# Extra products of two constants on TensorE in a fused transformer and expert kernel, and both heads' value products in one PSUM bank

## What is computed

```python
def first_block(x, c, ...):                        # in the kernel: ffn1 ... ffn2
    h = rms_norm(x, g_pre_ffn1) * (1 + sc1) + sh1
    x = x + 0.5 * gt1 * rms_norm(swiglu(h, ...), g_post_ffn1)
    u = rms_norm(x, g_pre_mix) * (1 + sc2) + sh2
    y = hybrid_mixer(u, ...)                       # index scores, dil and dsa attention, gates, w_o
    x = x + gt2 * rms_norm(y, g_post_mix)
    h = rms_norm(x, g_pre_ffn2) * (1 + sc3) + sh3
    return x + 0.5 * gt3 * rms_norm(swiglu(h, ...), g_post_ffn2)

# the index scores of a block of 128 queries, 8 heads of 32 features
logits = jnp.einsum('bqhe,bse->bqhs', qi, k_idx) * idx_scale
iscore = jnp.einsum('bqh,bqhs->bqs', wi, jax.nn.relu(logits))
_, sel = lax.top_k(where(causal, iscore, -inf), 128)       # the keys that dsa attends to

# each attention (dil, dsa, mla), per head and block of queries
p = softmax(where(mask, q @ k.T * scale, -inf)); o = p @ v

def second_block(x, c, ...):                       # in the kernel: in2 ... peer
    h = rms_norm_2(x, g_norm1) * (1.0 + sc1) + sh1
    mixed = concat(mla_group(h @ w_in ...), retention_group(...)) @ w_out
    x = x + gt1 * mixed
    h2 = rms_norm_2(x, g_norm2) * (1.0 + sc2) + sh2
    x = x + gt2 * peer(h2, w_query, sub_keys, expert_u, expert_v)
    return rms_norm_2(x, g_final)
```

## Time and profile before

| | us |
|---|---|
| median of three runs | 2976.38 |
| lowest and highest run | 2975.09, 2978.75 |
| span of the profiled execution, first to last instruction | 2975.7 |

### The profile page before, as it was taken

One profiled execution on the slowest core, in us unless ns is written; L12 is line 12 of the kernel. 1 busy time (PEld: TensorE's weight loads), 2 busy tenths in 40 slices (PEclk: granted clock), 3 DMA queues, 4 the chain that ended last, 5 costly groups with the idle time before them and its releaser, 6 DMA issues. The chain is left out here.

```text
span 2975.7 us, 37340 instructions
## 1 busy us (share of the span) xinstructions
PE 2827.2 (95%) x14083; PEld 2381.1 (80%) x14083; DVE 2012.1 (68%) x3510; ACT 1071.7 (36%) x1578; POOL 908.6 (31%) x603
## 2 busy tenths in 40 slices
PE   7999989888899999998989899999999999999998
PEld 6787878855687778887756789998899999898776
DVE  7754356376633783336445399899589888998887
ACT  3222232253523321223234335555433333333333
POOL 0000000040310000000014236676777777775230
PEclk9999999977999999999989999999999999999999
DMA  8963312101132873532111135665989898988994
GB/s 282 286 225 106 114 55 94 59 1 38 52 97 72 265 258 113 84 115 80 45 33 47 70 107 180 191 198 187 344 312 336 314 332 310 344 313 316 347 354 187
DMA packets 305769, 540.11 MB, mean 182 GB/s; under 512 B 19032, under 2 KB 199612, under 8 KB 287932
## 3 DMA queue, kind: packets, MB, share of 16 engines
q1 hardware_dynamic: 211936, 375.09, 37.5%
q0 software_dynamic: 36864, 134.23, 12.4%
q10 hardware_dynamic: 56796, 28.45, 3.5%
HBM read 498.90 MB, written 38.82 MB: 181 GB/s over the span
## 5 line engine op out<-in xcount | busy, mean ns | idle before, releaser
L183 PE MATMUL ps<-query_h_hi,expert_u_hi 128*128 128x384 f32 (+1 forms) x1152 | 399.5, 347 | 2.4 <-DVE query_h_lo L843 2.1
L183 PE MATMUL ps<-query_h_lo,expert_u_hi 128*128 128x384 f32 (+1 forms) x1152 | 395.5, 343 | 0.0
L2408 POOL TENSOR_TENSOR expert_u_lo<-feat,expert_u_hi 128x1024 fp32r<-128x1024 f32 x142 | 350.0, 2466 | 114.3 <-ACT expert_u_hi L2670 112.9
L183 PE MATMUL ps<-expert_v_hi,expert_w_hi 128*128 128x512 f32 x768 | 303.1, 395 | 8.3 <-DVE expert_w_lo L2576 5.8
L183 PE MATMUL ps<-expert_v_hi,expert_w_lo 128*128 128x512 f32 x768 | 301.2, 392 | 0.0
L183 PE MATMUL ps<-expert_v_lo,expert_w_hi 128*128 128x512 f32 x768 | 300.7, 392 | 0.0
L2581 DVE TENSOR_TENSOR expert_v_lo<-peer_s,expert_v_hi 128x1024 fp32r<-128x1024 f32 x128 | 204.5, 1598 | 121.3 <-ACT expert_v_hi L2678 120.5
L183 PE MATMUL ps<-ffn_h_hi,ffn_w_hi 128*128 128x512 f32 x704 | 279.2, 397 | 4.3 <-DVE ffn_h_lo L523 2.0
L183 PE MATMUL ps<-ffn_h_hi,ffn_w_lo 128*128 128x512 f32 x704 | 275.4, 391 | 0.0
L183 PE MATMUL ps<-ffn_h_lo,ffn_w_hi 128*128 128x512 f32 x704 | 275.3, 391 | 0.0
L246 DVE TENSOR_TENSOR ffn_w_lo<-ffn_w_raw,ffn_w_hi 128x2048 fp32r<-128x2048 f32 x64 | 146.6, 2290 | 158.4 <-ACT ffn_w_hi L230 158.4
(11 more groups left out here) (501 smaller groups left out, 6401.3 us busy)
## 6 DMA issues: line engine op xcount, KB each, us to landing
feat<-in_expert_u_blocks SPq DMA_DIRECT2D x64, 1024.0 KB
peer_s<-in_expert_v_blocks SPq DMA_DIRECT2D x64, 1024.0 KB
gate_rows<-expert_gates SPq DMA_DIRECT2D x31, 768.0 KB
ffn_w_raw<-in_w_down SPq DMA_DIRECT2D x22, 1024.0 KB, 5.0
ffn_w_raw<-in_w_gate SPq DMA_DIRECT2D x43, 512.0 KB, 7.5
ffn_w_raw<-in_w_up SPq DMA_DIRECT2D x43, 512.0 KB, 8.7
gate_rows<-in_w_mod SPq DMA_DIRECT2D x21, 1024.0 KB, 7.3
gate_rows<-in_w_ada SPq DMA_DIRECT2D x18, 1024.0 KB, 6.3
```

The source lines that it names most:

```text
L183: return nc.tensor.matmul(out, lhsT, rhs, start=start, stop=stop, skip_group_check=True)
L2408: nc.gpsimd.tensor_tensor(u_lo[:, n % 2, :, :], u_raw[:, n // 2 % 2, n % 2, :, :], u_hi[:, n % 2, :, :], ALU.subtract).then_inc(u_lo_done, 1)
```

## The change

`warm_up` becomes `keep_clock`, which issues n f32 products of the constants, 128 columns wide unless said otherwise, into a PSUM region that nobody reads at that time. It is called

- in `stage_norm_close` (three times in the program): 8 products ahead of the transposes of tile 2, 5 ahead of those of tile 3;
- in `stage_norm_queries`: 6 ahead of the transposes of tile 3 and 8 at the end;
- at the end of `stage_swiglu` (ffn1, ffn2) and of `stage_project_split` where the next stage is loaded early (o1, o2): 12, behind a wait for the PSUM bank to have been read;
- in the attention pairs (three times): after the scores of each of the first four pairs 4, 4, 1, 1 products of 256 columns in dil, one each in dsa and mla; and 6 of 256 columns at the end of TensorE's program;
- in the index scores: one after each of the 24 products, and 6 at the end.

Bank 7 becomes free for that in the attention by putting the values of both heads of a pair into bank 6.

```diff
-def warm_up(nc, b, n):
+def keep_clock(nc, b, n, bank, at=0, width=P):
...
     for _ in range(n):
-        mm(nc, b.ps[:, 7, :], b.const("identity"), b.const("decay_mask"), True, True)
+        mm(nc, b.ps[:, bank, at:at + width], b.const("identity"), b.const("decay_mask")[:, 0:width], True, True)
...
             for i in range(TT):
                 if i >= TT - 2:
+                    keep_clock(nc, b, 8 if i == TT - 2 else 5, DC - 1, S - P)
                     pe.wait_ge(norm.scaled, i - (TT - 2) + 1)
...
                 if i == TT - 1:
+                    keep_clock(nc, b, 6, DC - 1, S - P)
                     pe.wait_ge(norm.scaled, 1)
...
                 ins.then_inc(back, 1)
+            keep_clock(nc, b, 8, DC - 1)
...
+                pe.wait_ge(y_out, 8 + 2)
+                keep_clock(nc, b, 12, 0)
...
+                if early:
+                    pe.wait_ge(*((out_act, 1) if add_row is None else (out_dve, 1)))
+                    keep_clock(nc, b, 12, 0)
...
-            return b.ps[at:at + DV, 6 + n % 2, 0:P]
+            return b.ps[at:at + DV, 6, 0:P]
...
                     if p < NP:
                         scores(p)
+                    if p < 4:
+                        keep_clock(nc, b, (4 if p < 2 else 1) if width > S else 1, 7, 0, 2 * P)
                     if 0 <= p - 1 < NP:
                         turn(2 * p - 2)
                     if p >= 2:
                         values(p - 2)
                     if 0 <= p - 1 < NP:
                         turn(2 * p - 1)
+                keep_clock(nc, b, 6, 7, 0, 2 * P)
...
                        k_idx_t[at:at + 32, 0:(i + 1) * P], True, True).then_inc(up, 1)
+                    keep_clock(nc, b, 1, 7)
+                keep_clock(nc, b, 6, 7)
```

## The result

The changed kernel takes 3013.76 us (median of 4 runs, 3012.05 to 3016.49); the kernel before, on the same chip, 2976.07 (2975.09 to 2978.75). The ratio is 1.0125 with a 95% interval of [1.0113, 1.0137]: slower by 37.7 us, where 3010 was forecast.

A forecast was written before the change was run, and what follows sets the result against it. TensorE is busiest, often at half clock; DVE paces the index scores. Index +32, dil +5.5, dsa and mla +2, norms -3.5, nt5 +1.1 sum to +37, said as +34: 3010 us from 2975.7; range 2969 to 3020.

The forecast's parts named there:

- the +32 of the sum: Index scores: extra products on all 128 rows make items serial at half clock, +32 us; chance 0.66.
- the 0.3 us an item for the two changes between row groups: Index scores: switching between row groups and full array costs 0.3 us an item, bounds 0 and 0.52; 7.2 us.
- Shaving the sum of +37 to +34: Whole kernel: terms sum to +37 us, but some of the 0.3 for changes may hide under streams, so +34.
- Taken +5.5: Dil: pair 0 +0.7, pair 1 +1.2, pairs 2 and 3 +0.6, six products at the end +3 us.
- the 0 to 1.4 of the forecast: Dil, pair 0: four products take 1.8 to 3.4 us where TensorE idles 2.06; 0 to +1.4, taken +0.7.
- that uq's first product waits for the weights whatever happens ahead of it: Dil's end: the delay goes through whole, and faster transposition ahead of uq gives nothing back; +3 us.
- as counted (+2.0 and +1.9): Ends of dsa and mla: six products at full clock, 2.6 us, outlast ACT; +2.0 for dsa, +1.9 for mla.
- the whole of it and not half: Behind dsa and mla: next products at full clock could return 2.2 and 2.6 us; half counted, -1.1 and -1.3.
- Mla's start, taken at 0 within -3 to +3: Mla: one product behind each of the first four scores may bring its start out of 0.50 clock; 0 us.
- The counting of half: Norm stages: nothing fills the gap between last transposes and first products, so half the possible gain is counted, -3.5 us.
- the sign named as wrong: Norm stages: norm products still 0.43 us apart in the profile would show the prediction wrong.
- the stage at full clock: Rival: index scores run serially at full clock, stage +4 to +11, whole about 2987 us; chance 0.15.
- the gain that the other rival hoped for: Rival: DVE still paces index scores and first products run at full clock; net -8, 2968 us; chance faster 0.12.

The follow-up runs named there:

- the combined run: Kernel before plus products of norms, stage ends, mla's first four scores, starts of gated products and split of y; values in one bank: 2968.58 us, ratio 0.9973.
- the run on 32 rows: Changed kernel with each index score's extra product cut to 32 other rows, in its own bank, and without the six at that stage's end: 2979.05 us.
- the run with dil's products put back: Kernel before plus the combined run's products, dil's as in the change, and the 8 at the query norm's end: 2975.22 us, ratio 0.9995.
- the first four experiments: Apparently four edits of the changed kernel's index stage: products removed, 2981.80 us; on 32 rows, 2979.05; 26 products ahead, 3014.92; one pass each, 3009.35.

## Why the prediction was right, and which terms were off

**The index scores.** The mechanism was right at every step: serial items, half clock throughout, DVE waiting for TensorE. The term was mis-sized: +38.7 instead of the +32 of the sum. The step is the 0.3 us an item for the two changes between row groups, with 0.52 as its upper bound: they measured 0.59, each of them 0.3, a little more than the 0.26 that the earlier trace rows show bare. 24 times the difference is 7 us. Shaving the sum of +37 to +34, because some of it might hide under the streams, went the wrong way: nothing was hidden.

**Dil.** Taken +5.5. In the changed kernel +0.9 for the pairs and +3.1 for the end, less 1.1; against the combined run +5.1. The four products behind pair 0 lay in the wait in the changed kernel, as argued, but not in every run: on 32 rows and in the run with dil's products put back they came out of it by 1.1, within the 0 to 1.4 of the forecast. One step failed: that uq's first product waits for the weights whatever happens ahead of it. The transfer took 4.9 us from request to use before, but only 3.9 after:

```profile
718.81 3.97 PE L183 MATMUL ps<-consts 128*128 128x256 f32 x12
718.91 0.81 ACT L1783 ACTIVATE tok<-ps 64x128 f32<-64x128 f32 x2 [3.01 <-PE ps L183]
...
723.03 0.90 SPq L1245 DMA_DIRECT2D uq_w<-in_w_uq  x2
...
723.08 2.37 PE L1619 MATMUL ps<-consts,latents 128*128 128x128 f32 x20 [0.30 <-PEq L1682]
...
726.91 1.26 PEld L183 LDWEIGHTS ps<-uq_w,lat_t 128*128 128x128 f32 x5 [1.70 <-DMA uq_w<-in_w_uq]
```

In the kernel before, 3.9 us after the request would have been 686.0, while ACT's last copy of the transposes at half clock ended at 686.78:

```profile
686.09 0.69 ACT L1619 ACTIVATE lat_t<-ps,vec_cols 128x512 f32<-128x512 f32 x1 [0.39 <-PE ps L1611]
```

So the end of that stage set the start, not the weights; with the transposes at full clock (2.37 us for 20) 1.1 us came back. The delay by the six products, here 3.1, was as forecast.

**Dsa and mla.** The ends cost +2.2 each, as counted (+2.0 and +1.9). Returned were -2.1 and -2.5, the whole of it and not half; only in the run on 32 rows did the clock fall again among the first gated products, and 0.5 came back. Mla's start, taken at 0 within -3 to +3, gained 3.1 to 3.2, and 2.4 to 3.2 in the first four experiments; in the run with dil's products put back it was 1.0. So the two together gave -3.3 instead of +2.

**Norms.** -4.8 in the changed kernel (in1 -0.2, ffn2 -0.5, in2 -2.2, nt5 -1.9), where -3.5 was taken, but alone no gain that can be measured. The counting of half was the right way to see it; what one execution gains at in1 or in2 is not a property of the change. In in1 the sign named as wrong, products still 0.43 apart, did appear.

**The query norm's end** cost +1.0 (taken +1.1): TensorE's eight products outlast ACT, and the first request of the experts goes out at 1708.48:

```profile
1705.41 1.03 PE L886 MATMUL ps<-consts,feat 128*128 128x128 f32 x8
1706.05 1.08 ACT L838 ACTIVATE tok<-ps 128x512 f32<-128x512 f32 x2 [2.55 <-PE ps L886]
...
1706.29 1.95 PE L183 MATMUL ps<-consts 128*128 128x128 f32 x16
1708.48 0.38 SPq L2374 DMA_DIRECT2D gate_rows<-in_sub_keys  x1
```

**One bank, stage ends:** 0, as taken. Of the rivals, the stage at full clock was tried by entering it at full clock, and it fell back; the gain that the other rival hoped for is there, some 8 us, where products fill waits only. Why one execution's first norm products find the clock at half and the next's at full is left open.

**The sum.** That the whole came within 4 us of 3010 is in part luck. In the trace the index scores were 7 us dearer than taken; dil (+2.9 instead of +5.5), dsa and mla (-3.3 instead of +2) and the norms (-4.8 instead of -3.5) were together 9 cheaper, and the two misses largely cancelled.

## What to carry to other kernels

A product that nobody reads was free here where TensorE waited for something else and the product ended before that wait did, or where it ran on rows that its neighbours left free. Put it behind the barrier, in the wait, not ahead of the barrier where others wait for the block to end, and count its length at the lower clock. Before putting one between small products, look at how many of those are in flight at once: if their busy time is half the sum of their passes, they live from using different rows, and one product over all rows makes them serial. A higher mean clock is no gain by itself; here it rose from 0.968 to 0.977 with 38 us lost.

## What the hardware showed that was not expected

- Each change between a product on 32 rows and one on all 128 costs about 0.3 us at half clock (0.59 an item) and 0.2 at full (0.40 of 1.04), while 14 passes of one form in a row lasted 3.36 us, loads of weights included.
- TensorE busy for 57.80 of 58.10 us stayed at 0.50 throughout; entered at 1.00, the same stage fell to 0.50 within five items, without idling in between.
- 24 extra products on free row groups added nothing to the stage's 19.4 us, in which TensorE was already busy for 15.63 of 19.20.
